# A decoder layer on one core: the values of all heads by seven half-block products, their weights summed by adding transfers

## The reference, cut to what matters

```python
h = rmsnorm(x, norm_mix_pre)                       # 512 x 1024
proj = h @ w_in                                    # columns qA kA vA qR kR vR gR, 512 each
ya = moba_attention(qA, kA, vA, rel_bias); yr = retention(qR, kR, vR, gR)
x = x + rmsnorm(concat(ya, yr) @ w_out, norm_mix_post)
u = causal_conv3(rmsnorm(x, norm_ffn_pre) @ w_up)
x = x + rmsnorm((gelu(u_gate) * u_val) @ w_down, norm_ffn_post)
```

## Time and profile before

| | |
|---|---|
| median of 3 runs | 612.88 us (612.45 to 613.14) |
| the profiled execution | 612.64 us, span 610.8 us |
| TensorE products, busy | 601.1 us (98%), 3614 instructions |
| VectorE busy | 465.9 us (76%) |
| ScalarE busy | 359.8 us (59%) |
| GpSimd busy | 146.0 us (24%) |
| transfers | 94.40 MB, 155 GB/s over the span |
| granted TensorE clock | 0.998 of full speed |

### The profile page before, as it was taken

How to read it: one execution, slowest core, us unless ns; L and a number is a source line. 1 busy time by engine, 2 the same in 40 slices (tenths; PEclk the granted TensorE clock), 3 DMA queues, 4 the chain that set the end, 5 groups by cost and what they waited for, 6 DMA issues and landing times.

```text
span 610.8 us, 9406 instructions
## 1 busy us (share of the span) xinstructions
PE 601.1 (98%) x3614; PEld 524.1 (86%) x3614; DVE 465.9 (76%) x662; ACT 359.8 (59%) x563; POOL 146.0 (24%) x147
## 2 busy tenths in 40 slices
PE   8999999999999999999999999999999999999996
PEld 8888787787777868899999999999999988777884
DVE  4530377597696976888956689888999899999886
ACT  5432375575656844674834566666667656776561
POOL 4100231131331302421021231223123222432213
PEclk9999999999999999999999999999999999999999
DMA  8552423323323068680497988998899879997933
GB/s 318 175 147 60 140 69 106 102 69 104 104 70 104 34 207 275 203 244 4 104 215 126 188 174 150 217 196 171 148 223 194 171 139 184 164 221 180 229 113 137
DMA packets 81936, 94.40 MB, mean 155 GB/s; under 512 B 3082, under 2 KB 64186, under 8 KB 81891
## 3 DMA queue, kind: packets, MB, share of 16 engines
q0 software_dynamic: 26352, 35.15, 33.9%
q1 hardware_dynamic: 55538, 58.64, 29.4%
HBM read 91.66 MB, written 2.12 MB: 154 GB/s over the span
## 4 chain that ended last, share of the span: by engine, by line
PE 81%; DVE 13%; issue 2%; ACT 2%; POOL 0%; DVEq 0%; POOLq 0%; ACTq 0%
PE bank L710 72%; DVE ws L2000 4%; PE bank L786 2%; PE bank L843 2%; PE bank L739 1%; PE bank L721 1%; PE bank L831 1%; DVE hT L1973 1%; PE bank L775 1%; PE bank L774 1%; PE bank L821 1%; PE bank L820 1%; DVE yT L1973 1%; DVE work L1871 1%; DVE work L1990 1%
## 5 line engine op out<-in xcount | busy, mean ns | idle before, releaser
L710 PE MATMUL bank<-hT,ws 128*128 128x256 f32 (+1 forms) x1416 | 246.8, 329 | 0.2 <-DVE hT L1589 0.2
L710 PEld LDWEIGHTS bank<-hT,ws 128*128 128x128 f32 x1416 | 207.8, 190 | 21.8 <-issue 0.9
L710 PE MATMUL bank<-yT,ws 128*128 128x256 f32 x864 | 106.8, 283 | 0.0
L710 PEld LDWEIGHTS bank<-yT,ws 128*128 128x128 f32 x864 | 105.2, 192 | 0.2
L710 PE MATMUL bank<-ws,hT 128*128 128x512 f32 x432 | 100.4, 391 | 0.3 <-DVE ws L2000 0.3
L710 PEld LDWEIGHTS bank<-ws,hT 128*128 128x128 f32 x432 | 80.5, 188 | 17.9 <-DVE ws L2000 1.2
L710 PE MATMUL bank<-ws,yT 128*128 128x512 f32 x366 | 87.7, 394 | 0.3
L1571 DVE TENSOR_TENSOR ws<-raw,ws 128x1024 fp32r<-128x1024 f32 x47 | 58.8, 1252 | 30.3 <-ACT ws L1138 29.7
L710 PEld LDWEIGHTS bank<-ws,yT 128*128 128x128 f32 x366 | 67.3, 188 | 16.2 <-issue 1.9
L1409 ACT ACTIVATE ws<-raw 128x1024 fp32r<-128x1024 f32 x46 | 48.7, 1060 | 45.8 <-PE bank L710 45.7
L1138 ACT ACTIVATE ws<-raw 128x1024 fp32r<-128x1024 f32 x48 | 50.4, 1056 | 30.8 <-PE bank L710 26.6
(11 more groups left out here) (170 smaller groups left out, 766.0 us busy)
## 6 DMA issues: line engine op xcount, KB each, us to landing
raw<-in_w_in_dram SPq DMA_DIRECT2D x28, 512.0 KB, 3.8
raw<-in_w_up_dram POOLq DMA_DIRECT2D x27, 512.0 KB, 6.3
raw<-in_w_up_dram SPq DMA_DIRECT2D x23, 512.0 KB, 5.8
raw<-in_w_out_dram SPq DMA_DIRECT2D x16, 512.0 KB, 4.7
late<-in_w_up_dram SPq DMA_DIRECT2D x12, 512.0 KB, 6.6
raw<-in_w_down_dram POOLq DMA_DIRECT2D x12, 512.0 KB, 7.8
late<-in_w_up_dram POOLq DMA_DIRECT2D x9, 512.0 KB, 5.9
raw<-in_w_down_dram SPq DMA_DIRECT2D x9, 512.0 KB, 4.4
```

The costliest lines, as they stand in the source:

```text
L710: return nc.tensor.matmul(dst, st, mv, start=start, stop=stop, skip_group_check=onto)
```

## The change

The values are computed as a 2 x 2 by 2 x 2 block product: h is cut in two halves of rows (256) and two of k (512), the weights in two halves of k and the two column groups (vA, vR). Seven products of half blocks in place of eight give the four result blocks, in the order 1, 2, 3, 5, 6, 7, 4. Each product takes two weight tiles (g = 0, 1) and, for each, two row tiles x 3 parts x 2 k = 12 products of 128x512; there are 14 weight tiles.

- Weights: products 1, 2 and 3 use blocks as loaded; 5, 6 and 4 use the first block with one more block added each time, 7 uses the block of 3 with one added. GpSimd issues the eight adds (`add_values`), all in one order, tile 6 to tile 13, behind the statistics of the rows. Each waits for the low half of the tile that lay in the place before.
- Rows: products 1, 2 and 4 use the turned rows in `hT`; 3, 5, 6 and 7 use sums of blocks. ScalarE keeps the first two row tiles in full precision (`keep_rows`), VectorE makes the sums (`other_sums`, `fifth_sum`), ScalarE and VectorE split them into `yT` (`third_hi`, `sum_hi`, `sum_lo`).
- Results: ScalarE copies product 1 and the sum of products 1 and 2; VectorE makes the other blocks of the result out of PSUM by twelve instructions of 128x512 (`value_e`, `value_g`, `top_right`, `bottom_right`, `bottom_left`).
- Moves: x2 and x3 are loaded ahead of weight tile 1; weight tiles 2 to 5 follow at once. The high half of tile 0 comes behind the first turned rows on ScalarE. GpSimd clears `klA` and `klR` after the last value product. Some small tables move within `work`.

The core of the diff (helpers that only name a place, the smaller helpers of the sums and new semaphores are left out):

```diff
@@ -49,7 +49,15 @@
...
-VALUES = 8
+VALUE_ORDER = (1, 2, 3, 5, 6, 7, 4)
+VALUES = 2 * len(VALUE_ORDER)
+VALUE_BLOCK = {1: (0, 0), 5: (0, 1), 6: (1, 1), 4: (1, 0), 3: (1, 1), 7: (0, 1), 2: (1, 0)}
+VALUE_ADDED = (5, 6, 4, 7)
+VALUE_RAW = {1: (2, 3), 5: (2, 3), 6: (2, 3), 4: (2, 3), 2: (0, 1), 3: (4, 5), 7: (4, 5)}
...
@@ -495,36 +524,33 @@
...
+                sp.wait_ge(w_lo, lo_count(before_in_slot(n)))
...
+                sp.dma_start(value_raw(n).rearrange("p (k n) -> p k n", n=DMIX),
+                             value_block(n)).then_inc(raw_loaded[raw_slot_of(n)], 16)
 
             load_x(0)
             load_x(1)
             sp.dma_start(gains[:, 0, :], norm_mix_pre[0].partition_broadcast(P)).then_inc(gains_loaded, 16)
             load_values(0)
-            load_values(1)
             load_x(2)
             load_x(3)
+            load_values(1)
             load_values(2)
             load_values(3)
+            load_values(4)
+            load_values(5)
             sp.wait_ge(const_set, 2)
             sp.dma_start(relb[0:BUCKETS, :], rel_bias).then_inc(relb_loaded, 16)
             sp.dma_start(oneh, onehot).then_inc(oneh_loaded, 16)
             sp.dma_start(convrows[:, 0:3, :], conv_w[0].rearrange("j (t p) -> t j p", p=P)).then_inc(taps_loaded, 16)
             sp.dma_start(convrows[:, 3, :], conv_b[0].rearrange("(t p) -> t p", p=P)).then_inc(cbias_loaded, 16)
-            load_values(4)
             sp.dma_start(rot[:], rotary).then_inc(rot_loaded, 16)
-            for n in range(5, VALUES):
...
@@ -590,8 +616,6 @@
...
-            for low in (klA, klR):
-                nc.gpsimd.memset(low.bitcast(F32), 0.0).then_inc(low_cleared, 1)
...
+            def add_values(n):
+                c, before = raw_slot_of(n), before_in_slot(n)
+                pool.wait_ge(raw_loaded[c], 16 * loads_of_slot(n))
+                pool.wait_ge(lo_sem(before), lo_count(before))
+                pool.dma_start(value_raw(n).rearrange("p (k n) -> p k n", n=DMIX), value_block(n),
+                               accum_op=ALU.add).then_inc(raw_added[c], 16)
 
             x_rstd(0)
             x_rstd(1)
             split_lo(0)
             x_rstd(2)
             x_rstd(3)
+            for n in range(VALUES):
+                if is_added(n):
+                    add_values(n)
+            pool.wait_ge(unit_done, VALUES)
+            for low in (klA, klR):
+                nc.gpsimd.memset(low.bitcast(F32), 0.0).then_inc(low_cleared, 1)
+            pool.wait_ge(low_cleared, 2)
...
@@ -714,8 +753,9 @@
                 banks = H_BANK[t]
                 pe.wait_ge(h_rows, t + 1)
                 for half in range(2):
-                    if t == 3:
-                        pe.wait_ge(h_lo, 2)
+                    if t in (2, 3):
+                        pe.wait_ge(h_lo, 2 * t - 2)
+                        pe.wait_ge(v_kept, 2 * t - 2)
...
@@ -846,16 +886,31 @@
...
+            def value_rows(n, r, m):
+                _, p, g = unit_of(n)
+                c = slot_of(n)
                 for kk in range(2):
-                    k, cols = 2 * pair + kk, slice(kk * DMIX, kk * DMIX + DMIX)
-                    ins = three(bank[VALUE_BANK[side][t]][:], hT[:, 0, k, rows], hT[:, 1, k, rows],
-                                ws[:, slot_of(n), 0, cols], ws[:, slot_of(n), 1, cols], p,
-                                pair == 0 and p == 0 and kk == 0, pair == 3 and p == 1 and kk == 1)
+                    cols = slice(kk * DMIX, kk * DMIX + DMIX)
+                    if p in VALUE_SUM:
+                        k, rows = 2 * g + kk, slice(r * P, r * P + P)
+                        hi, lo = sum_block(p, 0)[:, k, rows], sum_block(p, 1)[:, k, rows]
+                    else:
+                        k, t = (0 if p == 1 else 4) + 2 * g + kk, r + (2 if p == 4 else 0)
+                        rows = slice((ST - 1 - t) * P, (ST - t) * P)
+                        hi, lo = hT[:, 0, k, rows], hT[:, 1, k, rows]
+                    ins = three(bank[VALUE_BANK[p][r]][:], hi, lo, ws[:, c, 0, cols], ws[:, c, 1, cols], m,
+                                p != 2 and g == 0 and m == 0 and kk == 0, g == 1 and m == 1 and kk == 1, p == 2)
                 return ins
+            def value_unit(n, r):
+                for m in (0, 2, 1):
+                    ins = value_rows(n, r, m)
+                if r == 1:
+                    ins.then_inc(unit_done, 1)
+                elif n % 2:
+                    ins.then_inc(v_first, 1)
...
@@ -864,39 +919,43 @@
             warm(2)
             turn_rows(1)
 
-            for n in range(2):
-                pe.wait_ge(w_hi, n + 1)
-                for t in range(2):
-                    pe.wait_ge(h_hi, 2 * t + 1)
-                    value_rows(n, t, 0)
-                    pe.wait_ge(h_lo, 2 * t + 1)
-                    value_rows(n, t, 2)
-                pe.wait_ge(lo_sem(n), lo_count(n))
-                for t in range(2):
-                    value_rows(n, t, 1)
+            pe.wait_ge(w_hi, 1)
+            for r in range(2):
+                pe.wait_ge(h_hi, 2 * r + 1)
+                value_rows(0, r, 0)
+                pe.wait_ge(h_lo, 2 * r + 1)
+                value_rows(0, r, 2)
+            pe.wait_ge(lo_sem(0), lo_count(0))
+            value_rows(0, 0, 1)
+            value_rows(0, 1, 1).then_inc(unit_done, 1)
             turn_rows(2)
-            pe.wait_ge(h_lo, 4)
-            pe.wait_ge(w_lo, lo_count(2))
-            for t in range(2):
-                for p in (0, 2, 1):
-                    value_rows(2, t, p)
+            pe.wait_ge(w_lo, lo_count(1))
+            value_unit(1, 0)
             turn_rows(3)
-            for t in (2, 3):
-                pe.wait_ge(h_lo, 2 * t + 2)
-                for n in range(3):
-                    for p in (0, 2, 1):
-                        ins = value_rows(n, t, p)
-                    if t == 3:
-                        ins.then_inc(unit_done, 1)
-            for n in range(3, VALUES):
-                pe.wait_ge(lo_sem(n), lo_count(n))
-                for t in range(ST):
-                    for p in (0, 2, 1):
-                        ins = value_rows(n, t, p)
-                ins.then_inc(unit_done, 1)
+            value_unit(1, 1)
+            for n in range(2, VALUES):
+                _, p, g = unit_of(n)
+                pe.wait_ge(w_lo, lo_count(n))
+                if p == 2:
+                    pe.wait_ge(h_lo, 4)
+                if p in VALUE_SUM:
+                    pe.wait_ge(s_lo, (3, 5, 6, 7).index(p) + 1)
+                if p == 6:
+                    pe.wait_ge(h_lo, 6)
+                if p in (7, 4):
+                    pe.wait_ge(h_lo, 8)
+                for r in range(2):
+                    if p == 2 and g == 0:
+                        pe.wait_ge(v_copied, r + 1)
+                    if p == 5 and g == 0:
+                        pe.wait_ge(v_corner, r + 1)
+                    if p == 4 and g == 0:
+                        pe.wait_ge(v_rows, r + 1)
+                    value_unit(n, r)
...
@@ -1140,6 +1199,8 @@
             def h_evacuate(t):
                 banks = H_BANK[t]
                 s = t % ST if t >= ST else ST - 1 - t
+                if t in (2, 3):
+                    act.wait_ge(s_sum, 3 * t - 4)
...
@@ -1162,27 +1223,84 @@
...
+            def keep_rows(t):
+                for half in range(2):
+                    act.wait_ge(h_lo, 2 * t + half + 1)
+                    nc.scalar.activation(hF[:, 4 * half:4 * half + 4, t * P:(t + 1) * P],
+                                         bank[H_BANK[t][half]][:].rearrange("p (k c) -> p k c", k=4),
+                                         ACT.Copy).then_inc(v_kept, 1)
...
+            def third_hi(r):
+                act.wait_ge(s_sum, 3 * r + 3)
+                here = slice(r * P, r * P + P)
+                nc.scalar.activation(sum_block(3, 0)[:, :, here], tF[VALUE_SUM[3]][:, :, here], ACT.Copy).then_inc(s_hi, 1)
+            def sum_hi(p):
+                act.wait_ge(s_sum, 7 if p == 5 else 6)
+                nc.scalar.activation(sum_block(p, 0), tF[VALUE_SUM[p]], ACT.Copy).then_inc(s_hi, 1)
 
             x_in(0)
             x_in(1)
-            split_hi(0)
             h_evacuate(0)
+            value_hi(0)
             h_evacuate(1)
-            split_hi(1)
             x_in(2)
             x_in(3)
-            split_hi(2)
+            keep_rows(0)
+            value_hi(1)
+            value_hi(2)
+            keep_rows(1)
+            value_hi(3)
+            value_hi(4)
+            first_copy_of_values(0)
+            first_copy_of_values(1)
+            third_hi(0)
+            third_hi(1)
+            value_hi(5)
+            corner(0)
+            sum_hi(5)
+            value_hi(6)
+            corner(1)
+            sum_hi(6)
+            value_hi(7)
             h_evacuate(2)
+            sum_hi(7)
             h_evacuate(3)
-            for n in range(3, VALUES):
-                split_hi(n)
-            value_copies(0)
```

(61 more changed lines are left out.)

117 lines of the change are left out of this document (85 added, 32 removed).

## The result

The changed kernel takes 615.85 us (615.1 to 616.06), the kernel before, run beside it, 612.54 us (612.38 to 613.14): 1.0047 times as long, with a 95% interval of 1.0034 to 1.0061. It is slower by 3.3 us. The forecast was 614.4 us within 611.8 to 617.2, with a chance of 0.57 for slower: the sign and the mechanism were right. Of the size, +1.7 us was forecast and +3.3 came, 1.6 us more.

What follows compares the result with a forecast made beforehand. TensorE, busy 601.1 of 610.8 us, was taken as the bound. -5.44 (products saved) + 6.16 (front) + 0.97 (tail) = +1.69 us on 612.64 gives 614.33, with the median's offset 614.6; 614.4 was given, range 611.8 to 617.2.

Steps and rivals of the forecast that it cites:

- What goes: Value stage on TensorE: 168 products in place of 192, a gain of 24 x 0.2267 = 5.44 us.
- front: Value stage up to the start of product 3: TensorE's waits there lose 6.16 us in all.
- walk: Hand count of each engine's queue in order from 10.62 us, giving TensorE's waits: 6.16 us ahead of product 3.
- Steps 1 and 2: First value products: tile 0's late halves lose 0.37 and 0.61 us; late rows hold the third turning, 1.28 lost.
- Steps 3 and 4: Behind the third turning, TensorE waits for the low halves of tiles 1 and 2: 1.15 and 0.80 us lost.
- Step 5: Behind product 2, TensorE waits for tile 4's low half, which stands behind sums on VectorE: 1.95 us lost.
- Step 6: The tail: adds land 2.6 us apart, add 13 at 52.2; TensorE waits in product 4, 0.97 us lost.
- bound of the text at 3.1 us an add: The tail, if adds beside plain loads take 3.1 us each: 1.0 to 2.5 us more lost.
- The clock: Rival: the clock falls during TensorE's waits, twelve products cost 2.72 us more, total 617; chance 0.05.
- rest of the kernel: Later key units: the value stage's shift passes on whole, with 0.8 us allowed either way.
- rival that the products come through: VectorE keeps up in the front: 610.6 us, with the tail 611.6; chance 0.12 for 607 to 611.7.
- weighed rule: GpSimd's statistics contend with VectorE: x3's may end at 18.9 harmlessly; were x2's caught too, the sum would be +2.5.

Runs made afterwards that it cites:

- plain run: Changed kernel with its eight adding transfers made plain transfers of the same bytes (weight blocks not summed): 613.35 us, 1.0013 times the kernel before.
- pair run beside each other: Changed kernel, and the same with weight tile 1 loaded ahead of x2 and x3 again, in one set: 616.39 and 616.40 us.
- exchange on VectorE: Changed kernel with the sum that frees product 4's second bank ahead of tile 13's low half: 614.82 us, 1.0036 times the kernel before.
- reordered kernel: Changed kernel's work, queues reordered in the value stage: 611.69 us (0.9991); 609.85 with key tiles 14, 15 held back and tile 6's add ahead of tile 7's.
- later sum: Changed kernel with tile 4's low half ahead of the fifth sum on VectorE: 616.88 us.

## Why the prediction came out as it did

- **What goes** (24 x 0.2267 = 5.44 us): right. The plain run, whose front loses what the walk said, is +0.63 for a walked +0.72.
- **Steps 1 and 2:** right. The high half of tile 0 starts at 11.20 (11.60 forecast, with a first turning 0.4 earlier), the third turning at 17.03 (17.30), released by VectorE's rows; the losses are 0.5, 0.7 and 1.3 for 0.37, 0.61 and 1.28. That early x2 and x3 buy nothing that can be measured was shown by the pair run beside each other.
- **Steps 3 and 4:** right: 0.84 and 0.73 for 1.15 and 0.80, and both released by low halves.
- **Step 5:** right: 1.93 for 1.95, with VectorE's queue on the chain. Its bracket is 1.64; read alone, it would make the walk look too high. The front as a whole: 6.1 us, forecast 6.16. From its first turning, product 3 starts at 20.90 for a forecast 21.13.
- **Step 6, the tail, is the term that was mis-sized:** 0.97 forecast, 3.0 measured (0.2 of it stands in the plain run too). The place is right (a wait in product 4 that VectorE ends), as these lines of after's chain in order of time show, the last of them ahead of the late products:

```profile
44.73 8.78 DMA raw<-in_w_in_dram
...
53.53 1.07 ACT ws L1235
...
54.62 1.23 DVE ws L1714
55.85 0.61 DVE xs L1765
```

The sum from the landing to the product holds too: 53.51 + 2.97 = 56.5, as forecast 52.2 + 2.97. What failed is the landing of add 13. It was forecast 52.2 - 9.98 = 42.2 us behind the first turning, and is 53.51 - 9.59 = 43.9. Of these 1.7 us, 0.5 are there at add 8 already (issued 0.25 later, landing in 6.0 for 5.8). The other 1.2 is the pace, 14.2 us for five landings, 2.84 apart and not 2.6. ScalarE's high halves of tiles 8, 9, 10 and 13 in after, each released by its landing:

```profile
39.33 1.06 ACT L1235 ACTIVATE ws<-raw 128x1024 fp32r<-128x1024 f32 x1 [2.72 <-DMA raw<-in_w_in_dram]
41.85 1.06 ACT L1235 ACTIVATE ws<-raw 128x1024 fp32r<-128x1024 f32 x1 [1.46 <-DMA raw<-in_w_in_dram]
45.38 1.06 ACT L1235 ACTIVATE ws<-late 128x1024 fp32r<-128x1024 f32 x1 [2.46 <-DMA late<-in_w_in_dram]
...
53.53 1.06 ACT L1235 ACTIVATE ws<-raw 128x1024 fp32r<-128x1024 f32 x1 [2.01 <-DMA raw<-in_w_in_dram]
```

The steps are 2.52, 3.53, 2.53, 2.55 and 3.07: three at the forecast rate and two longer ones. The transfers from 50 to 54 us (busy tenths of the 16 engines and GB/s in slices of 0.1 us) show what the last of them holds:

```profile
DMA  9999998998999993212111111000000000000000
GB/s 225 164 205 246 184 205 164 287 184 164 246 205 184 184 266 62 41 21 41 20 20 20 20 21 21 0 0 0 0 0 0 0 0 0 0 0 0 0 0 0
```

All engines are full up to 51.5, then for 1 us one to three tenths of their time still go, mostly at 20 to 40 GB/s, and the landing counts at 53.51, another 1.0 us on. The mean rate that I took from the earlier trace rows was right: from 38 to 50 us after moved 2.39 MB, 200 GB/s. What the rate says nothing of is when a landing counts, here 2.0 us behind the bulk. Why it counts late for some adds is open: the same thin end stands behind the last add in five other profiles, two of which have that landing 2.53 and 2.56 us behind the one before. With the bound of the text at 3.1 us an add (1.0 to 2.5 more than 0.97) the measured 3.0 lay within the range. The plain run shows that 2.8 of these 3 us hang on the late landings, and the exchange on VectorE that 1.0 to 1.8 of them came only with the order behind the last one.

- **The clock, and the rest of the kernel:** right. The grant over both halves of the stage, from the windows of after (the last three numbers are the granted clock, the busy share of the transfer engines and GB/s), is full:

```profile
12.00:31.00 19.00, 14.59 (x66) 10.85 (x67) 15.43 (x18) 14.47 (x23) 7.62 (x7) 1.00 0.96 258
31.00:60.70 29.70, 27.73 (x119) 21.87 (x119) 23.62 (x28) 14.94 (x18) 7.25 (x6) 1.00 0.73 142
```

- **The rival that the products come through** was priced at 610.6 to 611.6 for a VectorE that keeps up. The reordered kernel is that case, 611.69 as it stands and 609.85 at best, and it shows that work and room were there: what missed was the order. Its condition (9.0 us or less on VectorE between the ends of the low halves of tiles 1 and 4) was the right place to look. In after it is 30.44 - 18.68 = 11.8 us, as counted. In the reordered kernel it is 25.21 - 16.30 = 8.9, from these lines of VectorE (tiles 1 and 2, a low half every 1.14 us; tile 4):

```profile
15.08 2.36 DVE L1720 TENSOR_TENSOR ws<-raw,ws 128x1024 fp32r<-128x1024 f32 x2
...
23.99 1.22 DVE L1720 TENSOR_TENSOR ws<-late,ws 128x1024 fp32r<-128x1024 f32 x1
```

- **The weighed rule** (the Trainium skill, SBUF — State Buffer, "Who interferes with whom", that a GpSimd instruction which reads SBUF contends with a VectorE one with two inputs there): the first of x3's statistics took 1.29 us beside VectorE's row operation, for 0.19 for x2's, which met nothing, and did no harm. The trace agrees with the rule and with the sum.

## What to carry to other kernels

Before products are traded for sums and splits, walk the in-order queues from a fixed event up to the last landing; totals of idle time say little, and the same work in another order was about 6 us apart here (615.85 to 609.85). Don't attack the longest wait by itself: cutting it from 1.64 to 0.51 us made the kernel no faster, if anything slower, because a transfer behind it was issued later. Size a chain of transfers by their landings, not by their mean rate, and keep plain loads that nobody needs yet out of their way.

## What the runs showed of the hardware

- An adding transfer of 512 KB lands 5.7 to 6.6 us after its issue with little beside it, 10.0 us beside two plain loads in the reordered kernel, 8 to 11 us in a queue of adds; landings in a queue are 2.74 to 3.06 us apart on the mean of five in eight profiles, with single steps of 2.5 to 4.2. Why some steps are a microsecond or more longer than the others is open. GpSimd's issue of one takes 1.20 us, that of a plain transfer 0.72 us.
- The first turning falls between 9.19 and 10.62 us in 14 profiles, though the work ahead of it hardly differs. In four profiles VectorE, which had waited for the gains to land, is its last release (0.27 to 1.40 us waited); in the others the plain products ahead of it end last. I haven't tested what moves either. It is the reason for comparing stages and not starts.
- Two sets of runs of the change as it is differ by 0.54 us in the median (615.85 and 616.39), as much as some of the effects looked for; the kernel before moved by 0.4 at most (612.47 to 612.88). The exchanged tail, the plain adds and the later sum were compared with the change across sets. Their stages (-0.9, -2.8 and +1.4 us) come from one profile each, and one and the same kernel's stage moved by 0.07 in one pair of profiles (51.22 and 51.15) and by 0.94 in another (52.36 and 51.42). So the size of the first and the third is good to about a microsecond only; the waits that came and went are what the timelines show.
